# Rotary part of latent attention on 128 partitions, key copies on another engine, and projection chunks set singly beside attention pairs

## The reference, cut to what matters

```
proj = h @ w_in[l]          # dq dk dv | mq mk mv | c_q c_kv k_pe | g
oa = diff_attention(dq, dk, dv)        # 4 heads, each a difference of two softmaxes, then rms norm
ob = moba_attention(mq, mk, mv)        # 4 heads of 128
q  = rms(c_q) @ w_uq        # 8 heads x (64 plain + 32 rotary)
q  = concat(q[..., :64], rope(q[..., 64:], positions))
kv = rms(c_kv) @ w_ukv      # 8 heads x (64 key + 64 value)
k  = concat(kv[..., :64], rope(k_pe) broadcast to 8 heads)
oc = causal_attention(q, k, v)         # latent attention, "mla"
mixed = sum_g sigmoid(g_g) * (o_g @ w_branch[l, g])
rope(x) = x * cos + (half-swapped, sign-changed x) * sin
```

## Time and profile before

| | |
|---|---|
| median of 3 runs | 3192.73 us (3191.14 to 3193.69) |
| the profiled execution's own time | 3191.23 us |
| its span, first to last instruction | 3189.4 us |
| mean granted TensorE clock | 0.975 |
| layer 0, rotations to `gate20` | 2227.5 to 2400.8 us of the span |
| layer 1, the same | 2735.9 to 2909.2 us |

### The profile page before, as it was taken

One profiled execution on the slowest core, in us unless ns is written; L12 is line 12 of the kernel. 1 busy time (PEld: TensorE's weight loads), 2 busy tenths in 40 slices (PEclk: granted clock), 3 DMA queues, 4 the chain that ended last, 5 costly groups with the idle time before them and its releaser, 6 DMA issues. The chain is left out here.

```text
span 3189.4 us, 45761 instructions
## 1 busy us (share of the span) xinstructions
PE 3067.8 (96%) x18845; PEld 2684.9 (84%) x18845; DVE 1788.3 (56%) x3311; ACT 1173.2 (37%) x2009; POOL 77.6 (2%) x118
## 2 busy tenths in 40 slices
PE   7999999999999999999999998999999999999998
PEld 4788887888878888788887778999888999798998
DVE  1766664435558886643334444556655665656665
ACT  2322224333342222232223334444444544344443
POOL 1000000000000000000000000000001000001000
PEclk9899999999999999999998998999999999999999
DMA  8346452123125565622423323656235454435452
GB/s 275 99 141 177 141 164 95 42 85 99 61 85 173 175 200 176 187 76 83 112 68 108 95 81 87 192 166 196 80 113 179 154 188 129 124 93 172 135 185 91
DMA packets 501207, 421.28 MB, mean 132 GB/s; under 512 B 9946, under 2 KB 497674, under 8 KB 501000
## 3 DMA queue, kind: packets, MB, share of 16 engines
q1 hardware_dynamic: 497976, 412.33, 42.2%
q0 software_dynamic: 3024, 6.03, 0.8%
HBM read 417.20 MB, written 1.12 MB: 131 GB/s over the span
## 5 line engine op out<-in xcount | busy, mean ns | idle before, releaser
L1300 DVE TENSOR_TENSOR w_low<-raw,w_high 128x1024 fp32r<-128x1024 f32 (+2 forms) x720 | 761.7, 1099 | 352.6 <-ACT w_high L865 351.3
L865 ACT ACTIVATE w_high<-raw 128x1024 fp32r<-128x1024 f32 (+2 forms) x720 | 648.2, 949 | 673.5 <-PE gemm L1916 399.1
L1916 PE MATMUL gemm<-xh,w_high 128*128 128x512 f32 (+1 forms) x1792 | 675.2, 377 | 22.3 <-DVE xl L1336 22.3
L1916 PE MATMUL gemm<-xl,w_high 128*128 128x512 f32 (+1 forms) x1792 | 665.8, 372 | 0.0
L1916 PE MATMUL gemm<-xh,w_low 128*128 128x512 f32 (+1 forms) x1792 | 665.3, 371 | 0.0
L1916 PEld LDWEIGHTS gemm<-xh,w_high 128*128 128x128 f32 x1792 | 340.7, 190 | 92.4 <-issue 16.8
L1916 PEld LDWEIGHTS gemm<-xh,w_low 128*128 128x128 f32 x1792 | 340.9, 190 | 63.1
L1916 PEld LDWEIGHTS gemm<-xl,w_high 128*128 128x128 f32 x1792 | 341.5, 191 | 60.3 <-issue 0.2
L1916 PE MATMUL gemm<-yh,w_high 128*128 128x256 f32 x1216 | 351.8, 289 | 16.0 <-DVE yl L1361 7.1
L1916 PE MATMUL gemm<-yl,w_high 128*128 128x256 f32 x1216 | 346.6, 285 | 0.0
L1916 PE MATMUL gemm<-yh,w_low 128*128 128x256 f32 x1216 | 346.1, 285 | 0.0
(11 more groups left out here) (326 smaller groups left out, 4219.7 us busy)
## 6 DMA issues: line engine op xcount, KB each, us to landing
raw<-in_ffn_w_in SPq DMA_DIRECT2D x176, 512.0 KB, 5.3
raw<-in_w_mod SPq DMA_DIRECT2D x72, 1024.0 KB, 7.2
raw<-in_w_in SPq DMA_DIRECT2D x50, 1024.0 KB, 5.3
raw<-in_w_up SPq DMA_DIRECT2D x32, 1024.0 KB, 5.5
raw<-in_w_down SPq DMA_DIRECT2D x32, 1024.0 KB, 5.2
raw<-in_ffn_w_out SPq DMA_DIRECT2D x32, 768.0 KB, 4.6
raw<-in_ret_w_in SPq DMA_DIRECT2D x24, 1024.0 KB, 5.2
raw<-in_ffn_w_out SPq DMA_DIRECT2D x32, 640.0 KB, 4.2
```

Of the source, the lines that this page charges most:

```text
L865: act.activation(wh[i % SPL][:, a:b], raw[slot_of["w", i]][:, a:b], ACT.Copy).then_inc(w_high, 1)
L1300: dve.tensor_tensor(wl[slot][:, a:b], raw[slot][:, a:b], wh[i % SPL][:, a:b].bitcast(F32), ALU.subtract).then_inc(w_low, 1)
L1916: ins = pe.matmul(out, l_, r_, start=first and j == 0, stop=last and j == 2)
```

## The change: what it does

The query projection's columns are loaded in another order: first the 64 plain columns of all heads, then the 32 rotary columns of all heads, by four DMAs with runs of 256 and 128 bytes in place of one with runs of 3 KB. `mla_uq` then has ten chunks: eight of 64 columns and two of 128, each of these holding the rotary part of four heads on 128 partitions, in `yt`. Four 32-row matmuls on four row groups rotate one such tile; all eight stand before `mla_ukv`. DVE multiplies both tiles by sine and cosine on 128 partitions and adds into the heads' rows by four instructions. The angles, sine and cosine are made on 128 partitions. The seven key copies go to POOL. The projections beside the three attentions are run chunk by chunk, with a new formula and no lag, and `gate0`'s last two groups run beside moba attention.

```diff
-                                         [("A", 96 * i, 96) for i in range(MH)])],
+                                         [("A", 64 * i, 64) for i in range(MH)] + [("A", 512 + P * g, P) for g in range(2)])],
-                ... dst=lambda i: mq[0:96, i, :],
+                dst=lambda i: mq[0:64, i, :] if i < MH else yt[:, i - MH, :],
@@ alongside
-            na, nb = 2 * len(a.pairs), 24 if a.nat else 4 if a.kind == "dif" else 12
-            for x in range(na + 1):
+            for x in range(2 * len(a.pairs) + 1):
                 next(steps)
-                upto = min(nb, x - x // 13) if a.nat else 1 + x * (nb - 2) // na
+                upto = {"nat": min(24, x - x // 13), "dif": (x + 1) // 2, "mob": min(4, 1 + (x + 1) // 2),
+                        "mla": x + (x + 1) // 2}[a.kind]
@@ SP, load_block
+                if w == 768:
+                    heads = ap.rearrange("p k (h n) -> p k h n", h=MH)
+                    for k in range(nk):
+                        for at, a, b in ((0, 0, 64), (512, 64, 96)):
+                            to = dst[:, k, at:at + MH * (b - a)].rearrange("p (h n) -> p h n", h=MH)
+                            sp.dma_start(to, heads[:, k, :, a:b]).then_inc(raw_in[slot], 16)
+                    return
@@ POOL, before the sums of branch1 and branch2 of each layer
+                pool.wait_ge(roped, (MH + 1) * l + 1)
+                for hd in range(MH - 1):
+                    pool.tensor_copy(mk[64:96, hd, :], kpe[64:96, :]).then_inc(kpe_copied, 1)
@@ ACT (DVE and PE alike, except where shown)
-                alongside(f"diff{l}", attention(f"diff{l}"), both(*(gemm(o) for o in with_diff(l))), 1)
-                gate = gemm(f"gate0{l}")
+                alongside(f"diff{l}", attention(f"diff{l}"), both(*(gemm(o, by_chunk=True) for o in with_diff(l))), 0)
+                gate = gemm(f"gate0{l}", by_chunk=True)
-                run(attention(f"moba{l}"))
-                run(gate)
-                alongside(f"mla{l}", attention(f"mla{l}"), both(*(gemm(o) for o in with_mla(l))), 1)
+                alongside(f"moba{l}", attention(f"moba{l}"), gate, 0)
+                alongside(f"mla{l}", attention(f"mla{l}"), both(*(gemm(o, by_chunk=True) for o in with_mla(l))), 0)
@@ DVE
-            def rope(l, k):
+            def rope_queries(l, g):
+                dve.wait_ge(rot_x, 3 * l + 2 + g)
+                dve.tensor_tensor(yt[:, 2 + g, :], aux[g][:, 0:T], ang[:, 1, :], ALU.mult).then_inc(roped_part, 1)
+                dve.tensor_tensor(yt[:, g, :], yt[:, g, :], ang[:, 2, :], ALU.mult).then_inc(roped_part, 1)
+                dve.wait_ge(roped_part, 4 * l + 2 * g + 2)
+                for j in range(4):
+                    q = slice(32 * j, 32 * j + 32)
+                    dve.tensor_tensor(mq[R, 4 * g + j, :], yt[q, g, :], yt[q, 2 + g, :], ALU.add).then_inc(roped, 1)
                 steps = gemm(f"moba_q{l}")
-                rope(l, MH)
-                for k in range(4):
-                    rope(l, k)
+                rope_key(l)
+                rope_queries(l, 0)
                 next(steps)
-                for k in range(4, 8):
-                    rope(l, k)
+                rope_queries(l, 1)
                 run(steps)
-                for hd in range(MH - 1):
-                    dve.tensor_copy(mk[R, hd, :], kpe[R, :]).then_inc(roped, 1)
@@ PE
+                wait_gemm_out(pe, f"mla_uq{l}")
+                for g in range(2):
+                    for r in range(0, P, 32):
+                        ins = pe.matmul(aux[g][r:r + 32, 0:T], cst[r:r + 32, C_ROT:C_ROT + 32], yt[r:r + 32, g, :],
+                                        start=True, stop=True)
+                    ins.then_inc(rot_x, 1)
                 run(gemm(f"mla_ukv{l}", lambda kc: pe.wait_ge(x_low, C["p0"] + 3)))
-                (rotate(0..3), one group of moba_q, rotate(4..7), the other group)
+                run(gemm(f"moba_q{l}"))
-                pe.wait_ge(roped, 2 * MH * l + MH + 1)
+                pe.wait_ge(roped, (MH + 1) * (l + 1))
-                next(steps)
-                next(gate)
-                pe.wait_ge(sub_t, DH * (l + 1))
-                (the body of moba attention, then the last group of gate0)
+                alongside(f"moba{l}", behind_subln(attention(f"moba{l}")), gate)   # waits for sub_t after its first step
+                pe.wait_ge(kpe_copied, (MH - 1) * (l + 1))
                 pe.wait_ge(o_low, atts[f"moba{l}"].p1)
```

More of the change, by code:

```diff
@@ L62, in shape_constants @@
     inv = np.float32(10000.0) ** (-np.arange(16, dtype=np.float32) * np.float32(2.0) / np.float32(32))
[L63 to L67, removed]
+    for r in range(0, P, 32):
+        small[r:r + 16, C_INV] = inv
+        small[r + 16:r + 32, C_INV] = inv
+        for i in range(16):
+            small[r + i + 16, C_ROT + i] = -1.0
+            small[r + i, C_ROT + i + 16] = 1.0
     rel = 255 - np.arange(512)
@@ L374, in program @@
             two = kind == "w" and len(block_list[i][0].shape) == 4
-            counts[pos % RAW] += 32 if two else 16
+            by_head = kind == "w" and block_list[i][3] == 768
+            counts[pos % RAW] += 64 if by_head else 32 if two else 16
             slot_of[kind, i], value_of[kind, i] = pos % RAW, counts[pos % RAW]
@@ L1228, in _ @@
                 next(gate)
+                next(gate)
                 for hd in range(DH):
@@ L2260, in _ @@
                 wait_gemm_out(pe, f"diff_v{l}1")
-                alongside(f"diff{l}", attention(f"diff{l}"), both(*(gemm(o) for o in with_diff(l))))
-                gate = gemm(f"gate0{l}")
+                alongside(f"diff{l}", attention(f"diff{l}"), both(*(gemm(o, by_chunk=True) for o in with_diff(l))))
+                gate = gemm(f"gate0{l}", by_chunk=True)
+                next(gate)
                 next(gate)
@@ L2281, in _, with behind_subln @@
                 ins.then_inc(sub_row, 1)
-                steps = attention(f"moba{l}")
                 wait_gemm_out(pe, f"moba_v{l}1")
-                next(steps)
-                next(gate)
-                pe.wait_ge(sub_t, DH * (l + 1))
-                for x in range(2 * len(atts[f"moba{l}"].pairs)):
-                    next(steps)
-                run(steps)
-                run(gate)
-                pe.wait_ge(roped, 2 * MH * (l + 1))
+                def behind_subln(steps):
+                    yield next(steps)
+                    pe.wait_ge(sub_t, DH * (l + 1))
+                    yield from steps
+                alongside(f"moba{l}", behind_subln(attention(f"moba{l}")), gate)
+                pe.wait_ge(kpe_copied, (MH - 1) * (l + 1))
                 pe.wait_ge(sub_low, DH * (l + 1))
                 pe.wait_ge(o_low, atts[f"moba{l}"].p1)
-                alongside(f"mla{l}", attention(f"mla{l}"), both(*(gemm(o) for o in with_mla(l))))
+                alongside(f"mla{l}", attention(f"mla{l}"), both(*(gemm(o, by_chunk=True) for o in with_mla(l))))
                 for q in range(4):
```

53 lines of the change are left out of this document (22 added, 31 removed).

## The result

| | before | after |
|---|---|---|
| median | 3192.84 us (3191.14 to 3193.69) | 3169.01 us (3167.94 to 3171.19) |
| the profiled execution's own time | 3191.23 us | 3171.19 us |
| its span | 3189.4 us | 3168.7 us |
| mean granted TensorE clock | 0.975 | 0.977 |

The ratio is 0.9927, with a 95% interval of 0.991 to 0.9944: 23.8 us faster by the medians, 20.0 us by the two profiled executions, against which the sum of the prediction (-17.7) was made. The profiled execution of before lay 1.6 us under this median, that of after 2.2 us over its own.

The account below looks back on a forecast made before the run. PE, busy for 96% of the span, was taken as the bound. Layer 0's -8.8 and layer 1's -8.9 sum to -17.7 us on the profiled 3191.2: 3173.5 there, 3175.0 as a median, range 3164 to 3188.

Parts of the forecast that it names:

- signs of being right: Rotations within 3 us, about 3 us wait at second diff scores with half clock, under 0.5 us between pairs, about 1 before mla.
- Part 1: Rotations and rope: moba_q -8.8, eight rotations before mla_ukv +1.9, two more mla_uq chunks +1.4; -5.5 us per layer.
- a ratio from values on column halves: Rotations before mla_ukv: ratio 0.63 taken for overlap, giving 1.9 us for eight, between 0.74 and 3.0.
- Part 2: Diff attention's start: DVE's queue lets second scores start at T + 15.8, PE waits 3.2 us; +5.4 with half clock.
- so I count its 2.2 again: Behind the wait at diff attention's start: the half clock was expected to cost 2.2 us again.
- Part 3: Diff attention: a chunk beside each pair closes most waits; -4.8 us per layer, and 1.4 of half clock in layer 0.
- the four 0.3 us waits for ACT: Diff attention: where a chunk opens a group, ACT rounds weights before copying the turned tile; 0.3 us at four of eight pairs.
- Parts 4 and 5: Moba attention: idle +0.1 per layer, half clock +1.5 in layer 0; mla attention: three chunks per pair, -4.1 per layer.
- Costed at nothing: Key copies on POOL, the load in four DMAs, SP's three more issues and full-width angles were given no cost.
- The rival of the slow load: Query weight load in short runs lands late: at 48 us PE stands 15.5 us per layer, kernel 3206; chance 0.07.
- the clock holds: PE's new waits at diff start and in moba attention bring no half clock: 7.4 us less, 3167.6; chance 0.18.
- The waits move: Without lag, waits in diff and mla attention move instead of closing: 6.7 us per layer come back, 3188.4; chance 0.17.

Follow-up runs that it names:

- rotate_in_place: Changed kernel with 32 query rotations per layer in place of 8, four on one row group before the next: 3185.69 us, 0.9977.
- rotate_four_times: Changed kernel with each set of four query rotations issued four times over, going round the row groups: 3179.59 us, 0.9956.
- longer_rope: Changed kernel with four more chained DVE instructions in the rope of the first four heads, their values unread: 3175.92 us, 0.9944.
- late_split: Changed kernel with DVE's weight split ahead of the last two moba_q evictions left for the first diff chunk: 3164.87 us, 0.9912.
- copies_on_dve: Changed kernel with the seven key copies taken back from POOL to DVE, at their old place in the gate0 stage: 3168.25 us, 0.9921.
- moba_tail: Changed kernel with only three gate0 chunks inside moba attention, the fourth run after the attention's steps: 3173.67 us, 0.9935.
- start_chunk: Changed kernel with the first diff chunk already behind the first scores, every chunk of the stage half a pair earlier: 3183.49 us, 0.997.

## Why the prediction was right, and where it was off

The direction, the range and the mechanism hold: 3169.0 us lies in 3164 to 3188, and the waits that the prediction gave as its signs of being right are in the trace at their places. Smaller ones that it counted are not, and some are that it did not count. The point, 3175.0, was 6.0 us high by the medians and 2.3 us by the profiled executions. That small second number hides errors of both signs.

**Part 1** was -5.5 per layer, measured -5.8 and -5.9. The two extra chunks cost what was said (+1.4). The rotations with the key took 1.41 us in place of the key's 0.54, and `mla_ukv` behind them 0.3 longer, for DVE's weight split: +1.2 in place of 1.9. `moba_q` gave -8.4 in place of -8.8, for it ends in the 0.56 us wait for the rope. Two things were off in the rotations' price. One alone takes 0.43 us by the starts of its records and not 0.37 (four take 1.84 us in the earlier trace rows, from 2240.32 to the matmul at 2242.16), so eight one by one would be 3.4. And I had taken a ratio from values on column halves as the nearest row; `rotate_in_place` against `rotate_four_times` shows overlap four at a time to be nearer. By the Trainium skill ("TensorEngine Tiling (Array Packing)", Key Properties) tiles operate independently, and the trace agrees. Whether the change of tiling mode drains the engine doesn't show as more than 0.1 us at either end: the first rotation starts 0.21 us after the last 128-row matmul, where 0.12 is the pace, and the next 128-row matmul 0.30 us after the last rotation record, where 0.22 is.

**Part 2** was the count of DVE's queue. Predicted start of the second scores T + 15.8, measured T + 16.3 (2249.21 less 2232.95, the end of `mla_ukv`); predicted wait 3.2 us, measured 3.23 and 3.24. That the wait is right to 0.1 us is partly luck, since both of its ends came 0.4 to 0.5 us late: PE's by the 0.56 us wait for the rope. DVE was free at T + 2.05 in place of 2.4, and the sets of query ropes took 2.9 and 2.6 in place of 2.35: four adds from 32-row slices run 0.45 us apart, not 0.38, and 0.53 while POOL copies. `longer_rope` and `late_split` show that this queue is what decides, from both sides. The term that was mis-sized is "so I count its 2.2 again": the half clock came, but for 3.4 us and not 6.8, and cost 1.6 us by `copies_on_dve`. That is 0.6 too much per layer. `moba_tail` and both rotation experiments got 6.8 us at this place with the same wait, so the size was not to be had from one trace.

**Part 3** was -4.8 with the last tile in the open. Parts 2 and 3 together from first diff scores on: predicted -0.8 and +0.6, measured -2.0 and -0.5. Besides the clock, the four 0.3 us waits for ACT aren't there; two waits at the last two turned tiles are ([0.62] and [0.55]), 1.2 us in place of 2.1.

**Parts 4 and 5** together: predicted -2.5 and -4.0, measured -2.4 and -3.9. Here two errors cancel. Clock left out, moba attention gave -0.4 in both layers where I had +0.1 (three waits in place of four; the 0.5 for the first values isn't there). Layer 1's -2.0 holds the 1.6 us of half clock that went from there. Mla attention gave -2.0, 1.0 of it lost to the half clock that fell on its first scores, so -3.0 in place of -4.1: one wait for a turned tile is left, and not all of the 5.1 us was idle that a chunk can fill.

**What the prediction doesn't have**: the tail behind mla attention, -2.1 and -2.2. I read mla attention to its end and stopped; DVE's backlog at that point sets when the last projection can start. 1.0 us of it is the shorter wait, the rest the half clock behind it, 3.4 us in place of 6.8. This is the largest single miss, -4.4 us over both layers. The others are -0.7 in part 1, -2.3 in parts 2 and 3 and +0.2 in parts 4 and 5, and the clock in unedited parts gave +4.1 in this pair of profiled executions. These sum to -3.1 (-3.0 before rounding), by which the span's -20.7 passed the -17.7.

**Costed at nothing**: right for the load, wrong for the copies. On POOL they cost 0.6 us per layer by slowing DVE, as `copies_on_dve` shows; the prediction looked only at whether POOL had time for them. The load of `mla_w_uq` was issued and landed so in the changed kernel (SP's queue, and the issues of its weight with their median time to landing):

```profile
2181.40 5.61 SPq L784 DMA_DIRECT2D raw<-in_mla_w_uq  x4
```

```profile
raw<-in_mla_w_uq SPq DMA_DIRECT2D x4, 256.0 KB, 5.8
raw<-in_mla_w_uq SPq DMA_DIRECT2D x4, 128.0 KB, 4.7
```

Four issues hold SP for 5.61 us, 1.4 each and not 0.37, and the last transfer lands 8.1 us after the first issue, not 11. That is over twelve us before ACT reads the block at 2202.17, where it waits for PE. The rival of the slow load is out by that margin. By the Trainium skill ("DMA: Bandwidth & Descriptors", the table of properties) transfers under 512 B are below line rate. The whole block took 8.1 us where the one load with long runs took 6.7, but SP spent 5.6 us on the issues, so no run here shows whether the short runs themselves are slower.

**The rivals**: "the clock holds" was half true, and in `copies_on_dve` wholly so from the rotations to `gate20`, at 3162.4 us of span. "The waits move" didn't come here, but one half pair away, in `start_chunk`.

## What to carry to other kernels

When you chop cover into smaller pieces, list for every engine what stands in its queue between a piece and the next latency step. DVE took each chunk out ahead of the division that PE waited for; where PE had the next chunk to run meanwhile, that was hidden, and where it had only scores and values, the kernel lost 14.5 us to a shift by half a pair. When work that one engine did late becomes cheap for PE, count the other engine's queue to the first instruction that PE waits for; that count gave the size of the wait here. Work moved to an engine with time to spare isn't free if it slows a neighbour whose queue is on the path. And follow a change past the end of its stage, as far as the backlog it leaves reaches the next point where all engines meet.

## What the runs showed of the hardware that I had not expected

- The same wait (3.23 to 3.24 us) was followed by no half clock (`copies_on_dve`, which lacks the 0.56 us wait ahead of it), by 3.4 us (the changed kernel) or by 6.8 us (`moba_tail`, whose instructions up to there are the same), each alike in both layers. Waits of 1.0 to 1.4 us one behind another brought it too (the end of moba attention). So the clock's price read from one trace is a draw: 1.6 us for the first 3.4 us of it here, and 0.6 to 1.0 us more for the next 3.4.
- Four 32-row matmuls on four row groups overlap almost wholly: 0.11 us each against 0.25 for the same ones issued in place, where two groups work at once, and 0.43 for one alone.
- While POOL copied 32x256 tiles, DVE's adds of that size started 0.53 us apart and not 0.45, and two weight splits took 2.57 us and not 2.28.
- Four loads with runs of 128 and 256 bytes took SP 1.4 us each to issue, where one with long runs took 0.37.
